# Merge and output stages of a flow-matching layer: the third gated branch and the input row added by accumulating GpSimd transfers, sums one unit later, a fourth gating buffer

## The reference

```python
y_f = fourier_mix(u_f) @ w_proj_f_l
y_p = pool_mix(u_p, rows, w_pool_l, pool_scale_l) @ w_proj_p_l
y_m = (jax.nn.sigmoid(o) * hm) @ w_proj_m_l
g_f, g_p, g_m = jnp.split(jax.nn.sigmoid(merge), N_BRANCH, axis=-1)
y = (g_f * y_f + g_p * y_p + g_m * y_m) @ w_out_l
x = x + gate1 * rms_norm(y, norm_g_l[1])
h = rms_norm(x, norm_g_l[2]) * (1 + scale2) + shift2
a, b = jnp.split(h @ w_ffn_in_l, 2, axis=-1)
x = x + gate2 * rms_norm((jax.nn.silu(a) * b) @ w_ffn_out_l, norm_g_l[3])
```

## Time and profile before

| | |
|---|---|
| times of three runs | 1772.52, 1773.09, 1775.41 us; median 1773.09 |
| span of the profiled execution, first to last instruction | 1765.0 us |
| own time of the profiled execution | not given beside its span |
| PE busy | 1714.9 us (97%), 9622 matmuls |
| DVE busy | 910.0 us (52%) |
| ACT busy | 631.1 us (36%) |
| POOL busy | 222.9 us (13%) |
| clock granted to PE, mean | 0.996 of full speed |
| E1(0) to E2(2) | about 771 to 989 us of the span |

### The profile page before, as it was taken

The page is one execution under the profiler, slowest core; times in us unless marked ns, Lnnn a source line. Parts: engine busy times, 40 slices in busy tenths (PEclk is TensorE's granted clock), DMA queues, the critical chain, the costliest instruction groups (busy, mean ns, idle before and its releaser), DMA issues. The chain is left out here.

```text
span 1765.0 us, 24578 instructions
## 1 busy us (share of the span) xinstructions
PE 1714.9 (97%) x9622; PEld 1596.5 (90%) x9622; DVE 910.0 (52%) x1544; ACT 631.1 (36%) x1108; POOL 222.9 (13%) x340
## 2 busy tenths in 40 slices
PE   6999999999999999999899899999999999999997
PEld 3899999989999999998788799999999999888885
DVE  5400002343443444466868985555555553589785
ACT  6311113242222222234556672222222222354442
POOL 1400001322232233311100000000000000000000
PEclk9999999999999999999999999999999999999998
DMA  9554445764555566688857321222222225567683
GB/s 355 220 176 156 159 152 196 234 209 135 171 169 163 184 198 198 207 263 241 277 190 222 128 92 59 75 76 75 75 75 71 75 75 173 145 205 230 179 272 123
DMA packets 155289, 294.68 MB, mean 167 GB/s; under 512 B 12729, under 2 KB 91900, under 8 KB 155178
## 3 DMA queue, kind: packets, MB, share of 16 engines
q1 hardware_dynamic: 111312, 161.64, 28.3%
q0 software_dynamic: 27536, 91.31, 15.8%
q10 hardware_dynamic: 16336, 40.29, 6.4%
HBM read 225.42 MB, written 67.82 MB: 166 GB/s over the span
## 5 line engine op out<-in xcount | busy, mean ns | idle before, releaser
L664 PE MATMUL bank<-h_hi,w_hi 128*128 128x384 f32 x1080 | 373.8, 346 | 3.1 <-DVE h_lo L2609 2.6
L665 PE MATMUL bank<-h_lo,w_hi 128*128 128x384 f32 x1080 | 363.8, 337 | 0.0
L666 PE MATMUL bank<-h_hi,w_lo 128*128 128x384 f32 x1080 | 363.7, 337 | 0.0
L1948 DVE TENSOR_TENSOR w_lo<-raw,w_hi 128x1024 fp32r<-128x1024 f32 x152 | 185.3, 1221 | 241.2 <-ACT w_hi L1459 240.9
L664 PEld LDWEIGHTS bank<-h_hi,w_hi 128*128 128x128 f32 x1080 | 202.6, 188 | 20.3 <-ACT z_st L1519 10.1
L1459 ACT CAST w_hi<-raw 128x1024 fp32r<-128x1024 f32 x152 | 157.2, 1050 | 165.1 <-DMA raw<-in_w_stream 124.6
L665 PEld LDWEIGHTS bank<-h_lo,w_hi 128*128 128x128 f32 x1080 | 202.9, 188 | 0.1
L666 PEld LDWEIGHTS bank<-h_hi,w_lo 128*128 128x128 f32 x1080 | 202.5, 188 | 0.0
L666 PE MATMUL bank<-w_hi,a_lo 128*128 128x512 f32 x352 | 140.4, 399 | 0.0
L665 PE MATMUL bank<-w_lo,a_hi 128*128 128x512 f32 x352 | 138.7, 394 | 0.0
L664 PE MATMUL bank<-w_hi,a_hi 128*128 128x512 f32 x352 | 138.0, 392 | 0.0
(11 more groups left out here) (350 smaller groups left out, 3280.2 us busy)
## 6 DMA issues: line engine op xcount, KB each, us to landing
raw<-in_w_stream SPq DMA_DIRECT2D x142, 512.0 KB, 4.5
z_scratch<-z_st ACTq DMA_DIRECT2D x44, 576.0 KB, 3.1
raw<-in_w_stream SPq DMA_DIRECT2D x90, 256.0 KB, 4.1
raw<-in_w_ada SPq DMA_DIRECT2D x35, 512.0 KB, 5.9
mg<-z_scratch ACTq DMA_DIRECT2D x24, 576.0 KB, 6.3
a_raw<-f_scratch SPq DMA_DIRECT2D x44, 256.0 KB, 3.3
a_raw<-f_scratch SPq DMA_DIRECT2D x22, 320.0 KB, 3.2
zt<-z_scratch POOLq DMA_DIRECT2D x27, 256.0 KB, 4.0
```

What stands on the lines that cost most here:

```text
L664: pe.matmul(out, a_hi, b_hi, start=start, stop=False)
L665: pe.matmul(out, a_hi, b_lo, start=False, stop=False)
L666: return pe.matmul(out, a_lo, b_hi, start=False, stop=stop)
L1948: dve.tensor_tensor(w_lo[:, slot], raw[:, slot], w_hi[:, slot].bitcast(F32), ALU.subtract).then_inc(s_wlo, 1)
```

## The change

The sum of branch 0 and 1 stays with DVE. Branch 2 is now added to branch 1 in the `mg` buffer by a transfer that POOL issues after the gating, with addition at its destination (`third_branch`); DVE's one sum waits for that transfer and stands after the gating of the next unit, and `y_high` and `y_low` move one unit later too (the last ones into E2). `mg` gets a fourth buffer. `y_scale` writes into `xt` instead of `tb`, `x_add` is gone, and POOL's transfer adds the row of `xp_scratch` to `xt` (`x_sum`). Other semaphores that had reached their final counts are used again to count these transfers.

```diff
-MG, MX = 3, 2
+MG, MX = 4, 2
...
+        MG_BASE = (16, 16, 16, 1)
+        s_y2 = (s_wp, s_gl, s_st0, s_kvst)
+        Y2_BASE = (64, 32, 64, 16 * NT)
+        def x1_ready(eng, m):
+            eng.wait_ge(s_xl[m % 3], 16 * (NT + m // 3 + 1))
 # ACT
             def mg_load(x):
-                    act.wait_ge(s_ya, 2 * (x - MG + 1))
+                    act.wait_ge(s_ya, x - MG + 1)
             def x_square(m):
-                act.wait_ge(s_x1, m + 1)
+                x1_ready(act, m)
             def e1(g):
-                    if c:
-                        y_high(x - 1)
+                    if c >= 2:
+                        y_high(x - 2)
-                y_high(KT * g + KT - 1)
             def e2(g):
                     split(n + AHEAD, n + AHEAD)
+                    if k < 2:
+                        y_high(KT * g + KT - 2 + k)
 # DVE
             def y_scale(m):
+                if m >= 3:
+                    dve.wait_ge(s_x1s[m % 3], 16 * (m // 3))
+                    dve.wait_ge(s_xh, m - 2)
-                dve.scalar_tensor_tensor(tb[:, m % 3].rearrange("p (b n) -> p b n", b=2), ps[:, b:b + 2, :],
+                dve.scalar_tensor_tensor(xt[:, m % 3].rearrange("p (b n) -> p b n", b=2), ps[:, b:b + 2, :],
-            def x_add(m):
-                dve.tensor_tensor(xt[:, m % 3], xt[:, m % 3], tb[:, m % 3], ALU.add).then_inc(s_x1, 1)
+            def y_add(x):
+                dve.wait_ge(s_y2[x % MG], Y2_BASE[x % MG] + 16 * (x // MG + 1))
+                if x >= 2:
+                    dve.wait_ge(s_yl, x - 1)
+                dve.tensor_tensor(ya[:, x % 2], mg[x % MG][:, 0], mg[x % MG][:, 1], ALU.add).then_inc(s_ya, 1)
             def e1(g):
                     if g and c == 0:
-                        x_add(m)
                         y_scale(m + 2)
                     split(n + AHEAD, n + AHEAD)
 ...
                     dve.scalar_tensor_tensor(mg[x % MG], mg[x % MG], 1.0, ps[:, b0:b0 + 3, 0:GW], ALU.add,
                                              ALU.mult).then_inc(s_ym, 1)
                     if c:
-                        y_low(x - 1)
-                    dve.tensor_tensor(ya[:, x % 2], mg[x % MG][:, 0], mg[x % MG][:, 1], ALU.add).then_inc(s_ya, 1)
-                    dve.wait_ge(s_ya, 2 * x + 1)
-                    dve.tensor_tensor(ya[:, x % 2], ya[:, x % 2], mg[x % MG][:, 2], ALU.add).then_inc(s_ya, 1)
+                        y_add(x - 1)
+                    if c >= 2:
+                        y_low(x - 2)
                     if g == 1 and c in (5, 7):
                         b_low(c // 2 - 2)
-                y_low(KT * g + KT - 1)
             def e2(g):
+                    if k == 0:
+                        y_add(KT * g + KT - 1)
+                    if k < 2:
+                        y_low(KT * g + KT - 2 + k)
 # POOL
+            def third_branch(x):
+                pool.wait_ge(s_ym, x + 1)
+                pool.dma_start(mg[x % MG][:, 1], mg[x % MG][:, 2], accum_op=ALU.add).then_inc(s_y2[x % MG], 16)
+            def x_sum(m):
+                pool.wait_ge(s_yscale, 2 * m + 2)
+                pool.dma_start(xt[:, m % 3], xp_dram[tile_at(position(m))], accum_op=ALU.add).then_inc(s_xl[m % 3], 16)
             def e1(g):
+                for c in range(KT):
+                    if g and c == 0:
+                        x_sum(3 * g - 1)
+                    third_branch(KT * g + c)
+                    if g == 1 and c == 0:
+                        pool.wait_ge(s_new, 80)
+                    if g and 1 <= c <= 3:
+                        x1_store(3 * (g - 1) + c - 1)
+                    if g == 0 and c == 4:
+                        gains_load()
+                    if g < NG - 1 and c in (5, 6):
+                        mx_load_half(g + 1, c - 5)
-            def x_load(m):
-                pool.dma_start(xt[:, m % 3], xp_dram[tile_at(position(m))]).then_inc(s_xl[m % 3], 16)
             def e2(g):
-                for m in range(3 * g, 3 * g + 3):
-                    x_load(m)
                 ...
+                x_sum(3 * g)
+                x_sum(3 * g + 1)
             def fi():
                     if j == 0:
+                        x_sum(NT - 1)
                         for m in range(6, 9):
                             x1_store(m)
```

More of the change, by code:

```diff
@@ L383, in build @@
         mg01 = sb(s3g, "mg01", [P, 2, 3, GW])
-        sb(s3g, "mg_pad", [P, 3, GW])
+        mg3 = sb(s3g, "mg3", [P, 3, GW])
         mg2 = sb(s3g, "mg2", [P, 3, GW])
         s3g.close()
-        mg = (mg01[:, 0], mg01[:, 1], mg2[:])
+        mg = (mg01[:, 0], mg01[:, 1], mg2[:], mg3[:])
         B_raw["T1"], B_lo["T1"] = raw_and_low(s3t, "T1", [P, KH, GW])
@@ L451, in build @@
         s_mst = [sem(f"mix_stored{i}") for i in range(2)]
-        s_pmm, s_pa, s_pd, s_wp = sem("pooled"), sem("pool_act"), sem("pool_dve"), sem("w_pool_landed")
+        s_pmm, s_pa, s_pd, s_wp = sem("pooled"), sem("pool_act"), sem("pool_dve"), sem("w_pool_landed_or_third_branch_added")
         s_wp0 = sem("w_pool_zeroed")
-        s_gl, s_gp, s_gd, s_ga, s_gst = (sem(n) for n in ("gate_inputs_landed", "gate_pe", "gate_dve", "gate_act",
+        s_gl, s_gp, s_gd, s_ga, s_gst = (sem(n) for n in ("gate_inputs_landed_or_third_branch_added", "gate_pe", "gate_dve", "gate_act",
                                                           "g_rows_stored"))
         s_ld = [sem(f"chunk_landed{i}") for i in range(2)]
-        s_st0 = sem("state_landed")
+        s_st0 = sem("state_landed_or_third_branch_added")
         s_qk, s_int, s_iev, s_t, s_e, s_p, s_wv, s_intra, s_kvm, s_num, s_den, s_hd, s_cup = (
@@ L472, in build @@
         s_mxh, s_mxl = sem("mx_high"), sem("mx_low")
-        s_mg = [sem(f"merge_landed{i}") for i in range(MG)]
+        s_mg = [sem(f"merge_landed{i}") for i in range(3)] + [s_cz]
+        MG_BASE = (16, 16, 16, 1)
         s_ym, s_ya, s_yh, s_yl = (sem(n) for n in ("branches_gated", "y_summed", "y_high", "y_low"))
+        s_y2 = (s_wp, s_gl, s_st0, s_kvst)
+        Y2_BASE = (64, 32, 64, 16 * NT)
         s_g1 = sem("gain1_landed")
         s_xps = sem("x_with_pos_stored")
-        s_yt, s_ystat, s_yscale, s_x1, s_xstat, s_xrc, s_xh, s_xtt, s_h2r = (
-            sem(n) for n in ("y_tile_ready", "y_square_and_root", "y_rstd_and_scaled", "x1_ready", "x1_square_and_root",
+        s_yt, s_ystat, s_yscale, s_xstat, s_xrc, s_xh, s_xtt, s_h2r = (
+            sem(n) for n in ("y_tile_ready", "y_square_and_root", "y_rstd_and_scaled", "x1_square_and_root",
                              "x1_rstd", "x1_normed", "x1_turned", "h2_raw_ready"))
@@ L608, in scale_ready, with merge_landed @@
             eng.wait_ge(s_ostat, 2 * r + 2 + (2 if r >= 4 else 0))
+        def x1_ready(eng, m):
+            eng.wait_ge(s_xl[m % 3], 16 * (NT + m // 3 + 1))
+        def merge_landed(eng, x):
+            eng.wait_ge(s_mg[x % MG], MG_BASE[x % MG] + 16 * (x // MG + 1))
         def kind_of(q):
@@ L866, in x1_load @@
                     sp.wait_ge(s_x1s[CHAIN.index(r)], 16 * NG)
-                    sp.wait_ge(s_x1, NT)
+                    for m in range(6, NT):
+                        x1_ready(sp, m)
                 sp.dma_start(x1t[:, r % 3], x1_dram[FO_TILES[r]]).then_inc(s_x1l[r % 3], 16)
@@ L1683, in y_high @@
             def y_high(x):
-                act.wait_ge(s_ya, 2 * (x + 1))
+                act.wait_ge(s_ya, x + 1)
                 if x >= KT and x % KT == 0:
@@ L2265, in e1 @@
                     if g and c == 0:
-                        x_add(m)
                         y_scale(m + 2)
                     split(n + AHEAD, n + AHEAD)
-                    if g and c == 0:
-                        x_add(m + 1)
-                    elif g and c == 1:
+                    if g and c == 1:
                         x_rstd(m)
-                        x_add(m + 2)
                     elif g and c == 2:
@@ L2301, in t_step @@
                     dve.wait_ge(s_h2r, 6)
-                    dve.wait_ge(s_ya, 2 * NG * KT)
+                    dve.wait_ge(s_ya, NG * KT)
                 out, a, b, op = ((T1, B12, B11, ALU.subtract), (T1, T1, B11l, ALU.subtract),
@@ L2407, in fi @@
                         x_rstd(6)
-                        x_add(7)
                     if j:
@@ L2811, in x1_store @@
             def x1_store(m):
-                pool.wait_ge(s_x1, m + 1)
+                x1_ready(pool, m)
                 pool.dma_start(x1_dram[position(m)], xt[:, m % 3]).then_inc(s_x1s[m % 3], 16)
-            def e1(g):
[L2816 to L2827, removed]
-            def x_load(m):
[L2830 to L2835, removed]
-                pool.dma_start(xt[:, m % 3], xp_dram[tile_at(position(m))]).then_inc(s_xl[m % 3], 16)
+            def third_branch(x):
[4 more added lines that the diff above has]
+                pool.dma_start(xt[:, m % 3], xp_dram[tile_at(position(m))], accum_op=ALU.add).then_inc(s_xl[m % 3], 16)
+            def e1(g):
+                for c in range(KT):
[10 more added lines that the diff above has]
```

(3 more changed lines are left out.)

13 lines of the change are left out of this document (3 added, 10 removed).

## The result

The changed kernel takes 1786.45 us in the median (1782.74 to 1787.74, 4 runs), the kernel before 1774.25 beside it; the ratio is 1.0077, 95% interval 1.0059 to 1.0095. It is slower by about 13.7 us (0.0077 x 1773; by the interval 10.5 to 16.8). Forecast were 9.0 us less, with a range up to 1780: the prediction is wrong in sign and the time lies outside. The profiled execution took 1782.74 us, the shortest of the four; its span is 1781.0.

What follows compares the result with a forecast made beforehand. PE was taken as the bound, busy 97%, with 9.8 us of waits for DVE's gating to win. 4.5 + 1.3 + 2.5 + 0.7 = 9.0 us off 1773.1 gave 1764.1, likeliest 1761 to 1767, whole range 1760 to 1780.

Steps and rivals of the forecast that it cites:

- L: In E1, time from the end of a gating to the landing of its sum: taken 5.4 us, ends 2.5 and 7.9.
- the transfers behind others on POOL's queue: In E1(0), sums of transfers 5, 6 and 7 land late, L near 6, yet cost nothing; without cover 1 to 2 us.
- the 5.8 us of E1(1): In and behind E1(1), DVE no longer behind: waits fall from 7.0 to 2.5, winning 4.5 us, plus 1.3 of clock.
- E1(2): In and behind E1(2), PE's waits for gating fall from 2.8 to 0.3 us: 2.5 won.
- The bound, and where a gain could come from: PE is busy 97% of the span; its 9.8 us of waits for DVE's gating are most of what can be won.
- fi: In fi, x_turn's wait of 1.90 us loses the 1.13 input-row sum, less y_low's 0.47 in E2(2): 0.7 won.
- The recurrence of part 1: In E1, gating x+2 ends L + 3.5 after gating x; PE needs 8.33 us, so L up to 4.8 is free.
- rival (a): Behind E1(1), the hraw chain and clock loss stay because ACT is late, not DVE: 5.7 us won, 1768; chance 0.16.
- The input row: Three sums of 1.13 us leave DVE in each of E1(1), E1(2) and fi's first step; transfers land in 5 to 6.
- Rival (c): In E1, adding transfers meet full DMA engines and DVE stands in y_add: +9.3 us, 1782, for L above 6.6; chance 0.22.

Runs made afterwards that it cites:

- experiment 8: Both sums on VectorE one unit later, x_sum kept, plus ScalarE's y_high and gate load before h2_out and VectorE's gating before its split in E1(1): 1758.08 us, ratio 0.9912.
- experiment 4: The changed kernel with the 192 KB transfer as a plain copy instead of an adding one: 1777.44 us, ratio 1.0029 to the kernel before.
- experiment 6: The changed kernel with gate loads from the fifth unit on cut to one of three blocks: 1772.88 us, ratio 0.9998 to the kernel before.
- Experiment 1: The kernel before with only the input row added by a transfer (x_sum), branches summed by VectorE at once, three gating buffers: 1767.02 us, ratio 0.9968.
- experiment 3: The changed kernel with only the third-branch transfer undone: VectorE makes both sums one unit later, four buffers, x_sum kept; 1765.71 us, ratio 0.995 to the kernel before.
- Experiments 8 to 11: Two E1(1) order moves (ScalarE, VectorE) added to: experiment 3's kernel 0.9912, the changed kernel 1.0051, the kernel before 0.9974, experiment 1's kernel 0.9948.
- experiment 2: The changed kernel with the input row added by VectorE again, third branch still by transfer: 1786.14 us, ratio 1.0076 to the kernel before.
- experiment 7: The changed kernel with VectorE's order turned, the next split ahead of the sum that waits for the transfer: 1775.17 us, ratio 1.0012 to the kernel before.
- experiment 5: The kernel before with 18 more transfers, adding and plain, on POOL's queue in the quiet feed-forward stage; only landing times given, no kernel time.

## Why the prediction was wrong

The steps that failed are three: L, priced at 5.4 us; the transfers behind others on POOL's queue, put at nothing; and the 5.8 us of E1(1), laid on DVE's backlog. By stage, PE's waits for the gating were forecast and measured as follows: E1(0) 0 and 6.9, E1(1) 2.5 and 7.3, E1(2) 0.3 and 5.5. To the measured ones come two dips of the clock, 2.8 us.

- **The bound, and where a gain could come from**: right. PE's waits for the gating were most of what there was to win, and experiment 8 wins all but 1.1 us of them. Its 15.6 us are more than the 8.7 of waits, the 1.3 of clock and the 1.1 in fi that its trace accounts for; the rest is not located.
- **The recurrence of part 1** (gating x+2 ends L + 3.5 after gating x, L free up to 4.8): right. With L of 6.95 and 7.23 it gives 10.5 and 10.7 us for two units; 10.4 and 10.7 were measured.
- **L itself: the first step that failed.** The prediction took 0.3 + 4.5 + 0.6 = 5.4, and allowed up to 7.9. Measured were 6.6 to 7.2 in plain units of E1(0), and more where rows share POOL's queue: 8.5 in the first unit of E1(1), 8.7 in that of E1(2), 9.25 at the most. The 0.6 for the adding was near: 0.8 in quiet, about 1.0 in traffic. The 4.5 was too small: the plain copy took 5.9. Those loads were in traffic as heavy as E1's (the DMA engines busy 0.86, 288 GB/s at 745 to 768 us), so it isn't that their stretch was a quieter one; they came from DRAM and the copy stays within SBUF, and why it is slower is open. The case lay within their range, 2.6 to 7.6, and the median was taken for it. Each us of L above 4.8 is paid three times in each E1, less 2.8 of slack; in E1(0) this is PE's waits for the gatings 4 and 6, 3.4 us.
- **Transfers behind others in POOL's queue cost nothing: the second.** Wrong for y_add(5), and this is the other half of E1(0), 3.5 us. Its transfer stands behind the gains, and its sum started 9.1 us after its gating (799.28 to 808.40). I gave it slack that the even units had already used; gating 7 then ended 5.2 after gating 6, and PE stood 3.51. Experiments 4 and 6 part the two steps: with L near 5 in units 2 and 4 only the wait for gating 7 is left in E1(0), 3.0 and 4.9 us.
- **E1(1): 4.5 won from DVE's lost backlog, and 1.3 of clock: the third.** The prediction named its own test, b_low some 3 us earlier against product 5 if DVE's backlog was the cause. Experiment 1 took the three input-row sums away, and b_low starts 6.77 us after product 5 as before (863.93 to 870.70; before, 864.66 to 871.43). The long wait stayed at 4.5, in experiment 3 at 3.9. So "because DVE is behind" was a wrong reading: the trace before has DVE idle just ahead of this b_low, and again behind it, until ScalarE had made yy_hi (lines below). This is rival (a), whose chance was 0.16: ScalarE's y_high and the next weights stand behind h2_out. Experiments 8 to 11 show it. The 1.3 of clock stayed lost with it.

```profile
865.97 0.56 DVE L2229 TENSOR_TENSOR yy_lo<-ya,yy_hi 128x384 fp32r<-128x384 f32 x1 [1.31 <-ACT yy_hi L1687]
...
877.34 0.56 DVE L2229 TENSOR_TENSOR yy_lo<-ya,yy_hi 128x384 fp32r<-128x384 f32 x1 [2.22 <-ACT yy_hi L1687]
```

- **E1(2)**: 1.5 us of 2.8 are won by the input row alone (experiment 1) and all of them with the later sums (experiment 3); 2.7 are lost where the transfer is.
- **fi**: right. The turn waits 0.8 for 1.90, in the changed kernel and in experiments 1 and 3, so 1.1 us are won there where 0.7 were forecast.
- **The input row**: its gain came about, alone (5.7 us), and none that can be told when DVE has idle time to wait in anyway (experiment 2 against the changed kernel).
- **Rival (c)** was what happened, with its mechanism: DVE stands in y_add and PE waits in E1(0). Its prices were +6.5 in E1(0) (6.9 measured), +1.6 in E1(2) (2.7), +1.9 in E1(1) (0.3), and no clock dips. That 6.5 is so near 6.9 is luck: it was the slip at L = 7.9, while at the L that was measured the slip costs 3.4, and the other 3.5 come from the gains ahead on POOL's queue, which the rival did not price. It got 0.22 because the quantity that decides, a latency in traffic, was read from the median of another transfer and the point of turning, L of 6.6, was only 1.2 us away.

The Trainium skill, "DMA: Bandwidth & Descriptors", section "Issuing engines are not separate DMA queues", has the transfers of all issuing engines run on the same 16 DMA engines and interleave. Experiment 6 agrees: thinning the loads of ACT's queue brought the transfers of POOL's queue from 6.9 to 5.1 us. By the same page of the Trainium skill, in its anatomy of a GpSimd-issued DMA, 2.0 us plus the bytes at 436 GB/s give 2.45 for 192 KB, an estimate; the quiet plain copy took 2.3, the one in traffic 5.9.

Not settled: how the 3.8 us of traffic divide between POOL's own queue and the others'. Experiment 6 thinned ACT's loads alone and took 1.8 of them.

## What to carry to other kernels

An addition moved from an engine to a transfer trades half a microsecond of work for a latency. Before doing it, write down what stands behind the instruction that will wait, find the latency at which that begins to cost, and compare it with the longest, not the median, landing in the same stage with the new bytes in it; then look for each one of these transfers at what is issued ahead of it on its queue. If it has to be done, put the wait last in the unit (experiment 7 took back 11.5 of the 22.5 us that the transfer costs against DVE making both sums itself). And a stall that ends with one engine's instruction can be another's order: look at what the waiting chain passed through, and whether the engine that seems behind has been idle in it, before giving the stall to the busiest engine. Here the transfer was the wrong half of the change: the later sums and the input row without it, with two instructions moved, are 15.6 us faster than before.

## What the runs showed of the hardware that was not expected

- The row of an adding transfer on POOL is 0.93 us long where a plain one's is 0.54 (experiment 5), but the next transfer can be issued as soon: in the changed kernel the one behind an adding transfer starts 0.54 us after it, the step between the two plain gains in the trace before being 0.53.

```profile
796.23 0.86 POOL L2826 DMA_DIRECT2D mg<-mg  x1 [6.19 <-DVE mg L2293]
796.77 0.88 POOL L2817 DMA_DIRECT2D G1bc<-tab_scratch  x1
```

- An adding transfer lands 0.8 us (192 KB within SBUF) to 1.6 us (512 KB from DRAM) later than a plain one in a quiet stage (experiment 5).
- The same 192 KB transfer went from 3.1 us, with the DMA engines busy 0.26, to 6.9 in a stage where they were busy 0.88 before it was added and 0.97 with it.
- Over the thirteen traces PE's clock went to half (1.2 GHz) within 2 us after each of the 18 waits for the gating of 3.0 to 4.9 us. After the wait for `c_lo` in the first steps of fi, 2.5 us in all thirteen, it did so in nine and stayed full in four, the trace before among these. So a dip after a shorter wait belongs to the execution, not to the kernel, and two profiled spans can differ by several us through such dips alone.
